# Retention gates by exponentials and logarithms tile by tile, a later last sum and a later widening, and single-pass float32r products for the shift and the decay gates

## What is computed

```python
proj = x @ w_in                        # fq, fk, fv, f_logit, rq, rk, rv, rg
fox_out = fox_attention(fq, fk, fv, log_sigmoid(f_logit + b_forget))      # 8 heads of 64
ret = retention(rotary(rq), rotary(rk) * 128 ** -0.5, rv, gamma)          # 4 heads of 128
ret = (ret - mean(ret)) * rsqrt(var(ret) + 1e-5) * g                      # per head and token
mixed = concat(fox_out, silu(rg) * ret)
x = layernorm(ALPHA * x + mixed @ w_out)
x = layernorm(ALPHA * x + square(relu(x @ w_ff1)) @ w_ff2)
```

## Time and profile before

| | |
|---|---|
| median of 3 runs | 2051.24 us (2050.7 to 2051.36) |
| the profiled execution's own time | 2050.76 us |
| its span, first to last instruction | 2048.9 us |
| TensorE matmul busy | 2024.0 us, 99% |
| VectorE, ScalarE, GpSimd busy | 64%, 50%, 18% |
| granted TensorE clock, mean | 0.998 |

### The profile page before, as it was taken

One profiled execution on the slowest core, in us unless ns is written; L12 is line 12 of the kernel. 1 busy time (PEld: TensorE's weight loads), 2 busy tenths in 40 slices (PEclk: granted clock), 3 DMA queues, 4 the chain that ended last, 5 costly groups with the idle time before them and its releaser, 6 DMA issues. The chain is left out here.

```text
span 2048.9 us, 27766 instructions
## 1 busy us (share of the span) xinstructions
PE 2024.0 (99%) x11040; PEld 1730.9 (84%) x11040; DVE 1302.5 (64%) x2058; ACT 1020.7 (50%) x1684; POOL 371.3 (18%) x315
## 2 busy tenths in 40 slices
PE   9999999999999999999999999999999999999997
PEld 6888788888898998788788899898888788899896
DVE  6664656566774664476677575567677577566576
ACT  5664344334462543366357364464566357364363
POOL 0010000000133230254000233130354000323220
PEclk9999999999999999999999999999999999999999
DMA  7332222423232423633232242332533332242331
GB/s 245 98 108 64 83 62 83 143 95 111 90 117 73 133 66 100 181 103 103 98 104 85 81 144 62 105 122 63 166 110 90 115 93 95 65 143 62 124 104 41
DMA packets 201533, 211.58 MB, mean 103 GB/s; under 512 B 7803, under 2 KB 181115, under 8 KB 201404
## 3 DMA queue, kind: packets, MB, share of 16 engines
q1 hardware_dynamic: 194544, 194.13, 30.4%
q0 software_dynamic: 6352, 15.24, 2.8%
q10 hardware_dynamic: 508, 0.43, 0.1%
HBM read 194.55 MB, written 8.95 MB: 99 GB/s over the span
## 5 line engine op out<-in xcount | busy, mean ns | idle before, releaser
L686 PE MATMUL ps<-Phi,wh 128*128 128x512 f32 (+1 forms) x888 | 352.9, 397 | 3.8 <-DVE x_fvv L1359 1.3
L1273 DVE TENSOR_TENSOR wl<-stage,wh 128x1024 fp32r<-128x1024 f32 (+1 forms) x246 | 311.8, 1274 | 60.8 <-ACT wh L2135 42.1
L689 PE MATMUL ps<-Phi,wl 128*128 128x512 f32 (+1 forms) x888 | 332.1, 374 | 0.6 <-DVE wl L1273 0.6
L687 PE MATMUL ps<-Plo,wh 128*128 128x512 f32 (+1 forms) x888 | 331.4, 373 | 0.0
L2135 ACT ACTIVATE wh<-stage 128x1024 fp32r<-128x1024 f32 (+3 forms) x249 | 248.1, 1009 | 61.8 <-PE ps L689 38.9
L686 PE MATMUL ps<-Qhi,wh 128*128 128x512 f32 (+1 forms) x664 | 253.0, 381 | 0.7 <-DVE Qlo L1292 0.7
L687 PE MATMUL ps<-Qlo,wh 128*128 128x512 f32 (+1 forms) x664 | 251.6, 379 | 0.0
L689 PE MATMUL ps<-Qhi,wl 128*128 128x512 f32 (+1 forms) x664 | 251.5, 379 | 0.0
L2760 POOL TENSOR_TENSOR ws<-stage 128x1024 f32<-128x1024 f32 x20 | 54.9, 2744 | 932.2 <-PE ps L689 619.7
L686 PEld LDWEIGHTS ps<-Phi,wh 128*128 128x128 f32 x888 | 167.7, 189 | 41.0 <-issue 11.6
L689 PEld LDWEIGHTS ps<-Phi,wl 128*128 128x128 f32 x888 | 167.2, 188 | 31.8 <-DVE wl L1273 1.0
(11 more groups left out here) (357 smaller groups left out, 4579.2 us busy)
## 6 DMA issues: line engine op xcount, KB each, us to landing
stage<-in_w_ff SPq DMA_DIRECT2D x64, 1024.0 KB, 5.4
stage<-in_w_in SPq DMA_DIRECT2D x39, 1024.0 KB, 5.2
stage<-in_w_up SPq DMA_DIRECT2D x16, 1024.0 KB, 5.4
stage<-in_w_down SPq DMA_DIRECT2D x16, 1024.0 KB, 5.0
stage<-in_w_in SPq DMA_DIRECT2D x30, 512.0 KB, 5.2
stage<-in_w_out SPq DMA_DIRECT2D x12, 1024.0 KB, 5.0
stage<-in_w_bg SPq DMA_DIRECT2D x4, 1024.0 KB, 5.0
vrev<-H SPq DMA_DIRECT2D x2, 2048.0 KB, 14.4
```

Source lines behind the costliest of these rows:

```text
L686: e.matmul(o, hi[:, k, cs_], hi_x[:, kx, tok], start=k == 0, stop=False)
L687: e.matmul(o, hi[:, k, cs_], lo_x[:, kx, tok], start=False, stop=False)
L689: t = e.matmul(o, lo[:, k, cs_], hi_x[:, kx, tok], start=False, stop=k == nk - 1)
L1273: t = e.tensor_tensor(lo, src, hi.bitcast(F32), ALU.subtract)
```

## The change

1. **Gates of retention.** Instead of the sigmoid: for each rg tile ScalarE takes, right after the copy, the absolute value, exp(-|x|) and ln(1 + that); VectorE makes min(x, 0) minus it (`log_sigmoid`), ScalarE the exponential of the result (`sigmoid`, for tile j - 1, after the logarithm of tile j). VectorE multiplies with the gated output (`silu`). There are no table loads any more. Tiles 0 and 1 are split high within the last head's norm, the others after the last gemm.
2. **Last head's sum.** Two more empty turns before the last head's norm; the square of every head moves from the norm up to the output's turn.
3. **Widening.** `widen` comes after `two` instead of before it.
4. **Shift.** `centre` is made of H tile 0 alone (scale 8 instead of 4), copied as float32r, with the ones as float32r: one product in float32r.
5. **GLA gates.** The factors are laid out in 80 rows (high in rows 0 to 15, again at 32 or 64, low at 64 or 32, zeros between): one float32r product of 80 rows instead of a float32 product of 16. ScalarE makes four small copies and VectorE two subtractions and two fills once; GLA begins two turns later.

```diff
@@ tensor
-                on.wait_ge(gup_in["in"], vec_gla["low"], *free[4])
-                t = e.matmul(banks[4][:, :], gup[:, 128 * hd:128 * hd + 128], glow[:, :], start=True, stop=True)
+                on.wait_ge(act_gla["gup"], vec_gla["gup low"], act_gla["low"], vec_gla["low low"], *free[4])
+                t = e.matmul(banks[4][:, :], gup3[:, 128 * hd:128 * hd + 128], glow3[:, :], start=True, stop=True)
...
-                for _ in range(2):
+                for _ in range(4):
                     yield
                 for _ in gates(0):
...
-                on.wait_ge(vec_norm["acc", N, 1], *free[4])
-                t = e.matmul(banks[4][:, :], onec[:, :], accq[:, :], start=True, stop=True)
+                on.wait_ge(vec_norm["acc", N, 0], *free[4])
+                t = e.matmul(banks[4][:, :], onecr[:, :], first[:, :], start=True, stop=True)
...
                         norm = normed(h)
                         yield
+                    yield
+                    yield
                     for _ in norm:
...
-                w.mark("retained", L)
-                w.widen("wide", 1 + L)
...
                 w.two("Q", Qo, [frees((vec_x, ("ev",)))] * 2)
+                w.widen("wide", 1 + L)
@@ vector
+            e.memset(gup3[:, :].bitcast(F32), 0.0).then_inc(*vec_gla.up("gup zero"))
...
+            t = e.tensor_tensor(gup3[32:48, :], gup[:, :], gup3[0:16, :].bitcast(F32), ALU.subtract)
...
+            e.memset(glow3[:, :].bitcast(F32), 0.0).then_inc(*vec_gla.up("low zero"))
+            glow = tm1[0:16, :]
+            w.thin("P", nothing, ev_thin(glow, *turns_over(0)))
+            e.tensor_tensor(glow, glow, rB[0:16, :], ALU.mult).then_inc(*vec_gla.up("low"))
+            on.wait_ge(act_gla["low"])
+            t = e.tensor_tensor(glow3[64:80, :], glow, glow3[0:16, :].bitcast(F32), ALU.subtract)
...
-                    e.tensor_copy(accq[:, :], H[:, 0, :]).then_inc(*vec_norm.up("acc", N, 0))
+                    e.tensor_copy(first[:, :], H[:, 0, :]).then_inc(*vec_norm.up("acc", N, 0))
...
+                def log_sigmoid(j, L=L):
+                    on.wait_ge(act_ret["ln", "gate", L, j])
+                    t = e.scalar_tensor_tensor(out=sg[:, j, :], in0=rg[:, j, :], scalar=0.0, in1=sg[:, j, :],
+                                               op0=ALU.min, op1=ALU.subtract)
+                def silu(j, L=L):
+                    on.wait_ge(act_ret["sigmoid", L, j], vec_ret["gated", L, j])
+                    t = e.tensor_tensor(sg[:, j, :], sg[:, j, :], yr[:, j, :], ALU.mult)
...
                     w.gemm("P", 8, nothing, ev_rg)
+                    if j:
+                        log_sigmoid(j - 1)
                     gate()
+                    if j > 1:
+                        silu(j - 2)
                 w.finish()
+                gated_low(0)
+                gated_low(1)
+                silu(2)
                 gate()
...
+                log_sigmoid(3)
+                gated_low(2)
+                silu(3)
+                gated_low(3)
                 h_over[:] = [[back_in["in", L]] for _ in range(8)]
                 w.two("Q", nothing, (ev_down(0, ALPHA), ev_down(1, ALPHA)))
+                w.widen("wide", 1 + L)
@@ scalar
+                    if h == 3:
+                        gated_high(0)
+                        gated_high(1)
                     on.wait_ge(pe_ret["mean", L, h], vec_norm["consts"])
...
                         e.activation(rg[:, j, :], banks[b][:, :], ACT.Copy).then_inc(*act_x.up("ev", i, c))
-                        rg_over.append(act_x["ev", i, c])
+                        on.wait_ge(act_x["ev", i, c])
+                        e.activation(sg[:, j, :], rg[:, j, :], ACT.Abs).then_inc(*act_ret.up("abs", L, j))
+                        on.wait_ge(act_ret["abs", L, j])
+                        e.activation(sg[:, j, :], sg[:, j, :], ACT.Exp, scale=-1.0).then_inc(*act_ret.up("exp", "gate", L, j))
+                        on.wait_ge(act_ret["exp", "gate", L, j])
+                        t = e.activation(sg[:, j, :], sg[:, j, :], ACT.Ln, bias=1.0)
+                        t.then_inc(*act_ret.up("ln", "gate", L, j))
+                        if j:
+                            sigmoid(j - 1)
                     w.gemm("P", 8, nothing, ev_rg)
                 w.finish()
-                w.mark("retained", L)
-                for j in range(4):
-                    on.wait_ge(rg_over[j], *fox_over)
-                    e.activation(sg[:, j, :], rg[:, j, :], ACT.Sigmoid).then_inc(*act_ret.up("sigmoid", L, j))
...
-                e.preload_act_table_set("natural_log_exp_and_others")
-                w.widen("wide", 1 + L)
-                w.two("Q", nothing, (ev_down(0), ev_down(1)))
+                gated_high(2)
+                sigmoid(3)
+                gated_high(3)
+                w.two("Q", nothing, (ev_down(0), ev_down(1)))
+                w.widen("wide", 1 + L)
```

More of the change, by code:

```diff
@@ L591, in build @@
         rev = at("rev", g0 + 69, [128, 640])
-        glow = at("glow", g0 + 94, [16, 512])
+        glow3 = at("glow3", g0 + 94, [80, 512], F32R)
         go = at("go", g0 + 28, [128, 8, S])
@@ L614, in build @@
         acc2 = at("acc2", g0 + 70, [128, S])
+        first = at("first", g0 + 70, [128, S], F32R)
         cB = at("cB", g0 + 72, [128, S])
@@ L1469, in ev_thin @@
                 return evict
-            w.thin("P", nothing, ev_thin(glow[:, :]))
-            e.tensor_tensor(glow[:, :], glow[:, :], rB[0:16, :], ALU.mult).then_inc(*vec_gla.up("low"))
+            on.wait_ge(act_gla["gup"])
+            t = e.tensor_tensor(gup3[32:48, :], gup[:, :], gup3[0:16, :].bitcast(F32), ALU.subtract)
+            t.then_inc(*vec_gla.up("gup low"))
+            on.wait_ge(vec_gla["gup low"])
+            e.memset(glow3[:, :].bitcast(F32), 0.0).then_inc(*vec_gla.up("low zero"))
[4 more added lines that the diff above has]
+            t = e.tensor_tensor(glow3[64:80, :], glow, glow3[0:16, :].bitcast(F32), ALU.subtract)
+            t.then_inc(*vec_gla.up("low low"))
             on.wait_ge(*turns_over(0))
@@ L1756, in norm_tile @@
                     on.wait_ge(*h_over[0], *over("norm", N))
-                    e.tensor_copy(accq[:, :], H[:, 0, :]).then_inc(*vec_norm.up("acc", N, 0))
+                    e.tensor_copy(first[:, :], H[:, 0, :]).then_inc(*vec_norm.up("acc", N, 0))
                 else:
-                    on.wait_ge(*h_over[j], vec_norm["acc", N, j - 1], *([pe_sum["centre", N]] if j > 1 else []))
-                    e.tensor_tensor(accq[:, :], accq[:, :], H[:, j, :], ALU.add).then_inc(*vec_norm.up("acc", N, j))
+                    before = accq[:, :] if j > 1 else H[:, 0, :]
+                    on.wait_ge(*h_over[j], *([vec_norm["acc", N, j - 1]] if j > 1 else h_over[0]))
+                    e.tensor_tensor(accq[:, :], before, H[:, j, :], ALU.add).then_inc(*vec_norm.up("acc", N, j))
                 if j == 1:
@@ L2284, in scalar @@
                 w.gemm("P", 8, nothing, ev_val(j) if what == "val" else nothing)
+            on.wait_ge(gup_in["in"], vec_gla["gup zero"])
+            e.activation(gup3[0:16, :], gup[:, :], ACT.Copy).then_inc(*act_gla.up("gup first"))
+            e.activation(gup3[64:80, :], gup[:, :], ACT.Copy).then_inc(*act_gla.up("gup"))
             for half in range(2):
@@ L2288, in scalar @@
             w.thin("P", nothing, nothing)
+            on.wait_ge(vec_gla["low"])
+            e.activation(glow3[0:16, :], tm1[0:16, :], ACT.Copy).then_inc(*act_gla.up("low first"))
+            e.activation(glow3[32:48, :], tm1[0:16, :], ACT.Copy).then_inc(*act_gla.up("low"))
             def gates(hd):
@@ L2701, in retention @@
                         e.activation(yr[:, h, :], banks[6][:, :], ACT.Copy).then_inc(*act_ret.up("o", L, h))
+                        on.wait_ge(act_ret["o", L, h], *([vec_ret["y", L, h - 1]] if h else []))
+                        e.activation(wk[:, :], yr[:, h, :], ACT.Square).then_inc(*act_ret.up("square", L, h))
                         norm = normed(h)
                         yield
+                    yield
+                    yield
                     for _ in norm:
@@ L2713, in scalar, with sigmoid, ev_rg @@
                 w.pace = 0.66
-                rg_over = []
+                def sigmoid(j, L=L):
+                    on.wait_ge(vec_ret["log", L, j])
+                    e.activation(sg[:, j, :], sg[:, j, :], ACT.Exp).then_inc(*act_ret.up("sigmoid", L, j))
                 for j in range(4):
-                    def ev_rg(i, c, b, j=j, rg_over=rg_over, fox_over=fox_over):
+                    def ev_rg(i, c, b, L=L, j=j, fox_over=fox_over):
                         on.wait_ge(gemm["tile", i, c], *fox_over)
                         e.activation(rg[:, j, :], banks[b][:, :], ACT.Copy).then_inc(*act_x.up("ev", i, c))
-                        rg_over.append(act_x["ev", i, c])
+                        on.wait_ge(act_x["ev", i, c])
[7 more added lines that the diff above has]
```

(14 more changed lines are left out.)

24 lines of the change are left out of this document (12 added, 12 removed).

## The result

The changed kernel takes **2055.59 us** (median; 2053.56 to 2058.36) where the kernel before takes 2051.21 (2050.64 to 2052.05): the ratio is 1.0022, 95% interval 1.0015 to 1.0029. It is 4.4 us slower, 4.8 us above the forecast of 2050.8 and above its range, which ended at 2054.5. Its runs spread over 4.8 us, those of the kernel before over 1.4.

What follows compares the result with a forecast made beforehand. TensorE's queue was taken as the bound from end to end. Terms -3.7, -3.6, -1.8, +5.5, +0.9 and +2.3 sum to -0.4 on a base of 2051.2, giving 2050.8 us, range 2045.0 to 2054.5.

Steps and rivals of the forecast that it cites:

- masks' chain: Retention's gate tiles: four new activations delay weight high part, low part, masks and output; 0.6, 2.4 and 2.4 us.
- end of the gates: Last gate tile in the pair of output tiles: a longer chain makes TensorE wait, +0.9 us for both layers.
- last head's sum: Last head's norm in retention: two turns later, its sum no longer waits; 0.92 us gained per layer, -1.8 together.
- waits at the head's output: Product of the head's output in retention: TensorE starts late because masks come late, +5.5 us over both layers.
- linear attention's gates: GLA gate products become one float32r pass: 0.92 us gained at each of four, -3.7 us, without new waits.
- rival C: GLA two turns later: weight parts collide between gate and scores; 2058.4 us for four heads, 2054.6 for two; chance 0.08.
- The shift: Shift product in the norms: 0.63 us gained at norms 1 and 3, 1.19 at norms 0 and 2; -3.6 together.
- The widening: First mean of the norm's last three: one more low part made up there, 1.14 us per layer, +2.3.
- B: Retention's masks are not held up, or the waits swallow each other, so the +5.5 goes: 2045.3 us; chance 0.20.
- D: GLA gate and shift products are not single passes and keep their cost but for the wait: 2057 us; chance 0.03.
- E: Retention's gates: four table loads were on TensorE's path; removal gives 2048.7 us by rows, 2040.2 by page; chance 0.03.

Runs made afterwards that it cites:

- the first experiment: Changed kernel with the retention gates' absolute value, exponential, logarithm and previous tile's sigmoid put behind the next weight's high part (tiles 0 to 2): 2046.57 us, ratio 0.9979.
- changed again: The changed kernel itself, unedited, measured a second time beside the kernel with filled waits: 2055.84 us.
- ring as before: Changed kernel with the weight ring widened ahead of the two preparations, as in the kernel before the change: 2056.71 us, ratio 1.0029.

## Why the prediction was wrong

**Right, step by step.** Both products became single passes (the gate 0.23 of queue, the shift 0.23 where it starts on time). The masks' chain was read rightly in all three places: 0.71, 2.50 and 2.51 against 0.6, 2.4 and 2.4, and the first experiment shows by their removal that the activations ahead of the high part are the cause. The end of the gates (0.9 for 0.9) and the last head's sum of the earlier trace rows (1.9 for 1.8) stand.

**Wrong, the step that failed.** The waits at the head's output were priced at their own length: "Together **+5.5**". In these runs a wait of 2.44 or 3.13 us there was followed by half speed in four cases of eight, which cost 1.7 us each time. This term was missing. What it is worth on the median is known within bounds: filling the waits in part takes 3.4 us off (2055.84 to 2052.45), of which the traces give 2.2 to the filling, and the changed kernel's median lies 2.0 above its own lowest run. So 2 to 3.4 of the 4.8 us between forecast and result are this; with the waits filled the kernel stands 1.7 over the forecast, inside its range. The mis-sized terms come to 2.1 in the traces, which fits the rest.

**Mis-sized terms.** The linear attention's gates brought 2.5 and not 3.7: rival C's mechanism, given a chance of 0.08, came true in one head at 1.1 us and in another at 0.3, not between gate and scores but at the sum of squares behind them. Four new positions were taken to be free of collisions because the four old ones were. ScalarE, VectorE and TensorE there:

```profile
269.50 1.04 ACT L2168 ACTIVATE wh<-stage 128x1024 fp32r<-128x1024 f32 x1
...
270.65 1.23 DVE L1275 TENSOR_TENSOR wl<-stage,wh 128x1024 fp32r<-128x1024 f32 x1 [1.12 <-ACT wh L2168]
271.79 0.68 DVE L1556 TENSOR_TENSOR sq<-sq,sq 128x512 f32<-128x512 f32 x1
...
272.53 1.12 PE L932 MATMUL ps<-sq,onev 128*128 128x512 f32 x2 [1.07 <-DVE sq L1556]
```

The shift gave 3.4 for 3.6: 1.06 where 1.19 was taken for norms 0 and 2, since the copy is still a little late there, and 0.64 for the others, as forecast. The widening cost 2.9 for 2.3: in layer 0 the low part that is made up there also waits for its high part, 0.54 us at 1068.05 in the changed kernel (1.69 for 1.14), and in layer 1 it doesn't (1.22).

**The rivals.** B (masks not held up) is refuted by the waits. D is refuted by the single instructions. E, the four table loads on the path: the kernels without them (chain later, 2046.57) and with them (last head's sum and ring later, gates as before, 2046.54) are equal within the noise, so the new gates give TensorE nothing measurable back by doing without the loads. The page "ScalarE: Activation LUTs" of the Trainium skill (section "What ACT_TABLE_LOAD costs") gives some 2.66 us for a switch, by which four fewer are an estimated 10.6 us; nothing of that is seen here.

**Better than both.** The chain put later gives 2046.57, the shift and linear attention alone 2046.52, those with the later sum 2046.18, against 2050.9: 0.2% faster each, and not told apart from one another.

## What to carry to other kernels

When an operation is put into an engine's queue beside its eviction, look at what the planner issues next in that queue: here a weight's high part, on which VectorE and then TensorE waited, and moving the same work behind it turned +4.4 us into -4.3. Price a long new wait of TensorE (here 2.4 and 3.1 us) at more than its length, since its clock may be halved behind it, and look for that in the spread of the runs and in their granted clocks: a kernel whose runs suddenly lie 5 us apart has something that happens in some executions only. A positional argument ("no collision now") does not carry over to other positions.

## What the runs showed of the hardware

TensorE's waits of 2.09 to 3.13 us within the retention and the norm, of all thirteen profiles of changed kernels, and whether the granted clock behind them was 0.50:

| Wait | followed by half speed | not followed |
|---|---|---|
| 3.13 us, output, layer 0 | 1 (changed again) | 3 |
| 2.44 us, output, layer 1 | 3 | 1 (ring as before) |
| 2.09 to 2.99 us, first mean of the last three | 6 (2.09, 2.10, 2.12, 2.74, 2.90, 2.99) | 6 (2.13, 2.14, 2.17, 2.20, 2.44, 2.81) |

The length alone doesn't decide: the longest escaped three times of four, and 2.09 was caught. Five waits of 1.74 to 1.82 us at the first mean of norm 0 were not followed by half speed. Each stretch lasts 3.4 us, but for the one behind the wait of 2.90, which lasts 6.8. Behind an output one costs 1.7 us. Behind a mean it costs 1.2 to 1.6 at first (2.5 behind the 2.90), and 1.0 to 1.4 of that comes back at the next waits, so that 0.2 is left, and 1.1 behind the 2.90. The page "TensorE: Matmul & The Clock Gate" of the Trainium skill (section "What's actually happening") describes a clock gate that falls to 1.2 GHz by default when the engine has not been busy, and whose looking is not tied to the start of the kernel. That the same wait in the same kernel is caught in one execution and not in the next agrees with it.
